# A two-layer trunk on one core: token groups of three tiles and two, a third expert pick begun between merge steps, first queries in two passes, and three gates of four on ScalarE in the expansion

## The reference, cut to what matters

```
x = LN(alpha*x + g1 * (sum_n sigmoid(h @ Wgate_n) * (branch_n @ Wbranch_n)) @ Wout)   # n = 3 branches
h = LN(x) * (1 + sc2) + sh2
q = h @ peer_wq                       # 8 heads x 2 halves x 64
sv, si = top_k(q . subkeys, 16)       # per head and half, 128 keys each
cand = sv[0][:,None] + sv[1][None,:]  # 256 sums, the 16 best are the experts
gates = softmax(best 16)
out = sum over 8*16 experts of gate * gelu(h . u[e]) * v[e]
x = LN(alpha*x + g2 * out)
```

## Time and profile before

| | us |
|---|---|
| median of 3 runs | 4697.08 (4692.81 to 4699.29) |
| profiled execution, its own time | 4696.58 |
| its span, first to last instruction | 4694.8 |
| PE busy | 4083.7 (87%) |
| DVE busy | 3542.0 (75%) |
| ACT busy | 1482.1 (32%) |
| POOL busy | 2014.6 (43%) |

### The profile page before, as it was taken

One profiled execution on the slowest core, in us unless ns is written; L12 is line 12 of the kernel. 1 busy time (PEld: TensorE's weight loads), 2 busy tenths in 40 slices (PEclk: granted clock), 3 DMA queues, 4 the chain that ended last, 5 costly groups with the idle time before them and its releaser, 6 DMA issues.

```text
span 4694.8 us, 67028 instructions
## 1 busy us (share of the span) xinstructions
PE 4083.7 (87%) x23702; PEld 3584.3 (76%) x23702; DVE 3542.0 (75%) x6464; ACT 1482.1 (32%) x2065; POOL 2014.6 (43%) x1123
## 2 busy tenths in 40 slices
PE   6889999763799999999888999997448999999996
PEld 5866888753699888988777678887337988889885
DVE  2407447689899999999952263487898999999998
ACT  2226322222333332333232363232223333333331
POOL 1200313000287777877622004120004887778774
PEclk9999999887999999999988999998789999999998
DMA  5220332332699999999853104323228999999996
GB/s 219 108 96 1 135 148 99 131 108 81 223 401 403 383 394 372 408 394 396 329 199 135 51 19 153 130 108 127 84 81 311 403 396 398 393 373 405 389 396 250
DMA packets 334645, 1130.38 MB, mean 241 GB/s; under 512 B 26368, under 2 KB 124720, under 8 KB 277104
## 3 DMA queue, kind: packets, MB, share of 16 engines
q0 software_dynamic: 151168, 552.73, 30.4%
q1 hardware_dynamic: 83312, 519.61, 28.2%
q10 hardware_dynamic: 99968, 55.58, 3.9%
HBM read 1068.30 MB, written 59.51 MB: 240 GB/s over the span
## 4 chain that ended last, share of the span: by engine, by line
DVE 34%; PE 29%; POOL 10%; DVEq 10%; issue 9%; DMA 6%; ACT 2%; ACTq 0%; SPq 0%; POOLq 0%
PE PS L703 8%; DVE acc L2182 6%; DVE ring_lo L2152 5%; POOL got_a L678 5%; POOL got_b L678 5%; PE PS L712 4%; PE PS L713 4%; PE PS L714 4%; DVE ohB L2133 3%; DVEq L2174 3%; DMA ring<-weights 3%; DVE spare L2182 3%; PE PS L707 3%; DVEq L2159 3%; DVE got_b L2179 2%
## 5 line engine op out<-in xcount | busy, mean ns | idle before, releaser
L1509 ACT CAST ring_hi<-ring 128x2048 fp32r<-128x2048 f32 x256 | 489.7, 1913 | 1266.9 <-DMA ring<-weights 1266.9
L678 POOL DMA_INDIRECT got_a<-u_rows,sidx x256 | 426.5, 1666 | 866.0 <-DMA gate_matrix<-stg 768.2
L712 PE MATMUL PS<-hT_hi,ring_hi 128*128 128x384 f32 x2048 | 688.7, 336 | 14.2 <-DVE ring_lo L2152 14.2
L714 PE MATMUL PS<-hT_hi,ring_lo 128*128 128x384 f32 x2048 | 688.3, 336 | 0.0
L713 PE MATMUL PS<-hT_lo,ring_hi 128*128 128x384 f32 x2048 | 687.4, 336 | 0.0
L712 PE MATMUL PS<-ring_hi,W_hi 128*128 128x512 f32 x1536 | 607.5, 396 | 51.3 <-DVE W_lo L2168 51.3
L656 POOL TENSOR_TENSOR ring_lo<-ring,mhi 128x2048 fp32r<-128x2048 f32 x48 | 223.5, 4655 | 902.3 <-ACT mhi L1347 902.3
L713 PE MATMUL PS<-ring_lo,W_hi 128*128 128x512 f32 x1536 | 604.1, 393 | 0.0
L714 PE MATMUL PS<-ring_hi,W_lo 128*128 128x512 f32 x1536 | 604.1, 393 | 0.0
L2152 DVE TENSOR_TENSOR ring_lo<-ring,ring_hi 128x2048 fp32r<-128x2048 f32 x256 | 585.2, 2287 | 0.0
L678 POOL DMA_INDIRECT got_b<-v_rows,sidx x256 | 427.1, 1669 | 160.7 <-DVE acc L2182 90.2
(11 more groups left out here) (365 smaller groups left out, 8497.9 us busy)
## 6 DMA issues: line engine op xcount, KB each, us to landing
ring<-weights SPq DMA_DIRECT2D x444, 1024.0 KB, 7.7
G<-gate_matrix SPq DMA_DIRECT2D x128, 384.0 KB, 9.1
gate_matrix<-stg ACTq DMA_DIRECT2D x10, 4096.0 KB, 15.9
gate_matrix<-stg ACTq DMA_DIRECT2D x2, 3584.0 KB, 18.1
x_wait<-x POOLq DMA_DIRECT2D x2, 2560.0 KB, 23.0
x<-x_wait ACTq DMA_DIRECT2D x10, 512.0 KB, 10.0
lnr<-lnrows POOLq DMA_DIRECT2D x4, 1024.0 KB, 5.1
got_a<-u_rows,sidx POOLq DMA_INDIRECT x256, 9.0
```

Of the source, the lines that this page charges most:

```text
L678: pool.indirect_dma_start(out=got[n % GB], out_offset=None, in_=u_rows[:, :] if phase % 2 == 0 else v_rows[:, :], in_offset=bass.IndirectO ...
L712: mm(out, a_hi, b_hi, start=first, stop=False)
L714: return mm(out, a_lo, b_hi, start=False, stop=final)
L1509: nc.scalar.copy(ring_hi[s][:, :], ring[:, s, :]).then_inc(hi_ready, 1)
```

## The change

- The groups become three tiles and two: `TILES = ((0, 1, 2), (3, 4))`, so the first group has 384 columns and the second 256.
- In the second group gate and branch product of a merge share one bank, and merges 0 to 3 use banks 0 to 3 and need no `gated` between them. All four run before the transposes of the first group.
- Tile 2 joins tiles 0 and 1: its transposes, queries and scores are made inside the second group's merges. The first queries go in two passes over the same four weight blocks: tile 0 alone (128 columns), then tiles 1 and 2 (256). Only one pass (`WQB`, tiles 3 and 4) is left after the merges, and `WQC` with its four transfers is gone.
- On DVE the steps of the picks are numbered through (`hidden(n)`, 11 per tile). Steps 0 to 5 run after merge 3, 6 and 7 after merge 4, then one per merge. After merge 20 tile 2 has had steps 0 to 2; its steps 3 to 9 and `chosen` come after the second group's projection and normalisation.
- The copies of tiles 0 and 1 back to token order (`tokens_first`) move to merges 8 and 12.
- In the expansion DVE makes `ohB` with one comparison for three tokens and one compare-and-multiply for the fourth; ACT multiplies the three by their gates, two quads ahead of the copy (`gate_quad`). `ohB` has four buffers, so DVE may be four quads ahead of PE. PE waits for ACT's gates instead of DVE.

```diff
-TILES = ((0, 1), (2, 3, 4))
-FIRST = (0, 2)
-COLS = (2 * P, 3 * P)
+TILES = ((0, 1, 2), (3, 4))
+FIRST = (0, 3)
+COLS = (3 * P, 2 * P)
...
-                        for k in range(4):
-                            token = bass.ds(i * 16 + (4 * u + k), 1)
-                            last = ts_(ohB[:, u % 2, k, :], iota, idxT[:, 1, token], idxT[:, 2, token], ALU.is_equal, ALU.mult)
-                        last.then_inc(oh_ready, 1)
+                        others = idxT[:, 1, bass.ds(i * 16 + (4 * u + 1), 3)].unsqueeze(2).broadcast_to([P, 3, P])
+                        tt(ohB[:, u, 1:4, :], iota.unsqueeze(1).broadcast_to([P, 3, P]), others, ALU.is_equal)
+                        token = bass.ds(i * 16 + 4 * u, 1)
+                        ts_(ohB[:, u, 0, :], iota, idxT[:, 1, token], idxT[:, 2, token], ALU.is_equal, ALU.mult
+                            ).then_inc(oh_ready, 1)
...
+                        def gate_quad(i, q):
+                            act.wait_ge(oh_ready, l * N_QUAD + t * QUADS + i * 4 + (q + 1))
+                            for k in range(1, 4):
+                                token = bass.ds(i * 16 + (4 * q + k), 1)
+                                o = ohB[:, q % 4, k, :]
+                                last = A(o, o, ACT.Identity, scale=idxT[:, 2, token])
+                            last.then_inc(gated_ready, 1)
...
+                        with act.Fori(0, 4 - half) as i:
                             for u in range(4):
-                                act.wait_ge(quad_full, l * N_QUAD + t * QUADS + i * 4 + (16 * half + u + 1))
-                                nc.scalar.copy(st[:, :, bass.ds(i * 16 + 4 * u, 4)],
-                                               bank(4 + u).rearrange("p (t j) -> p j t", t=4)).then_inc(quad_ready, 1)
+                                gate_quad(i, 16 * half + u + 2)
+                                quad_out(i, u)
...
+                def hidden(n):
+                    t, b = n // 11, set_a
+                    step = n % 11
+                    if step == 0:
+                        best_eight(t, b, early)
+                    if step in (1, 2):
+                        found_eight(b, early, step - 1)
...
                 for j in range(24):
                     gated(1, j)
...
+                    if j == 3:
+                        for n in range(6):
+                            hidden(n)
+                    if j == 4:
+                        hidden(6)
+                        hidden(7)
+                    if 5 <= j < 13:
+                        hidden(j + 3)
+                    if j == 13:
+                        hidden(16)
+                    if j == 14:
+                        hidden(17)
+                        hidden(18)
+                    if 15 <= j < 21:
+                        hidden(j + 4)
...
+                for n in range(25, 32):
+                    hidden(n)
+                chosen(2, set_c, idx[:, 2, :]).then_inc(idx_ready, 1)
...
                 for j in range(24):
                     merge(1, j)
...
-                    if j == 1:
+                    if j == 3:
                         pe.wait_ge(row_ready, layer_at(l, 2, 2))
-                        ln_turn(1, xn2, TILES[0])
...
+                        ln_turn(1, xn2, (0, 1))
+                        pe.wait_ge(hT_ready, layer_at(l, N_HT, NT + 2))
+                        queries(WQA, 0, slice(0, P))
+                        pe.wait_ge(mg_done, layer_at(l, N_MG, 24 + 4))
+                        ln_turn(1, xn2, [2])
                         pe.wait_ge(q_ready, layer_at(l, N_Q, 4))
                         pe.wait_ge(keys_full, 16 * (l + 1))
                         score_early(0)
+                        pe.wait_ge(hT_ready, layer_at(l, N_HT, NT + 6))
+                        queries(WQA, 4, slice(P, 3 * P))
+                        pe.wait_ge(q_ready, layer_at(l, N_Q, 8))
+                        score_early(1)
```

More of the change, by code:

```diff
@@ L160, with group_of, out_step @@
     pm: object
+def group_of(t):
+    return 0 if t in TILES[0] else 1
+def out_step(group, k):
+    return (0, 4 * len(TILES[0]))[group] + len(TILES[group]) * k
 def layer_at(l, per_layer, n):
@@ L381, in bank, with ln_bank, query_at, merge_banks @@
             return PS[:, b * 512 + a:b * 512 + e]
+        def ln_bank(part, t, h):
+            return 4 + (2 * t + h) % 4 if part == 0 else (6, 4, 2, 0, 2)[t] + h
+        def query_at(j, size):
+            if j < 4:
+                return 6 + j // 2, 2 * size * (j % 2)
+            return (2 + j % 2 if j < 8 else j % 4), 0
+        def merge_banks(group, j):
+            n = COLS[group]
+            if group == 0:
+                return bank(2 * (j % 2), 0, n), bank(2 * (j % 2) + 1, 0, n)
+            b = j if j < 4 else j % 2
+            return bank(b, 0, n), bank(b, n, 2 * n)
         slot_full = [sem(f"slot_full{i}") for i in range(RING + 1)]
@@ L510, in trunk @@
             else:
-                last_use += merges[:HALF] + [(q_full, N_Q, k + 1) for k in range(4)] + merges[HALF:] + outs
+                last_use += merges[:HALF] + [(q_full, N_Q, 4 + k + 1) for k in range(4)] + merges[HALF:] + outs
         last_use += [(sc_full, NT, NT)]
-        last_use += [(q_full, N_Q, 4 + k + 1) for k in range(8)]
+        last_use += [(q_full, N_Q, 8 + k + 1) for k in range(4)]
         assert len(last_use) == PEER
@@ L1919, in _ @@
                 merged_lo(0, 7)
-                for j in range(8):
-                    if j == 6:
+                for j in range(12):
+                    if j == 9:
                         dve.wait_ge(ln1_rows, 16 * (l + 1))
@@ L2078, in pick @@
                     return chosen(t, set_b, gates)
+                def hidden(n):
[5 more added lines that the diff above has]
+                        found_eight(b, early, step - 1)
+                    if step == 3:
+                        next_eight(b)
+                    if step == 4:
+                        found_next(b)
+                    if step == 5:
+                        pair_sums(b)
+                    if step == 6:
+                        pairs_found(b)
+                    if step == 7:
+                        pairs_next(b)
+                    if step == 8:
+                        places(b)
+                    if step == 9:
+                        looked_up(t, b)
+                    if step == 10:
+                        listed(t)
@@ L2120, in _ @@
-                for t in others:
+                aggregate(TILES[1])
+                inverse_root(11, TILES[1])
+                for t in TILES[1]:
                     normalise(t, xn2[:, t - FIRST[1], :]).then_inc(xn_ready, 1)
-                with dve.Fori(0, ND) as t:
-                    pick(t + NS, idx[:, 2, :], l * ND + t + 1).then_inc(idx_ready, 1)
+                for n in range(25, 32):
+                    hidden(n)
+                chosen(2, set_c, idx[:, 2, :]).then_inc(idx_ready, 1)
```

261 lines of the change are left out of this document (124 added, 137 removed).

## The result

Before: 4698.18 us median (4692.81 to 4699.58, 4 runs). After: 4672.34 us (4666.48 to 4675.41, 4 runs). The ratio is 0.9946, 95% interval 0.9928 to 0.9963: faster by half a per cent. The profiled execution has a span of 4673.6 us against 4694.8, 21.2 less.

A forecast was written before the change was run, and what follows sets the result against it. DVE and PE were taken as nearly full in the merges, DVE as setting the expansion's pace. Terms summed to -11.8 us per layer, -23.6 for two, from 4696.6 to 4673 us; range 4640 to 4716.

The forecast's parts named there:

- Part 1, merges of group one: First group with three tiles: 24 merges at 6.74 us instead of 4.60, less one stall; +47.2 us per layer.
- Part 1, projection: First group's projection: 12 slices instead of 8, at 2.88 us each; +11.5 us per layer.
- Part 2, to merge 4: End of first projection to second group's merge 4, now with two query passes: +7.1 us per layer.
- Part 3, merges 4 to 23: Second group's merges, set by DVE's work plus stalls, not PE alone: -23.3 us per layer.
- Part 4, to the first one-hots: Merge 23 to the expansion: earlier, shorter projection and one query pass, 93.2 us for 129.5; -36.3 per layer.
- Part 5, expansion: Expansion quads at 1.38 us instead of 1.63, with three products on ACT: -18.0 us per layer.
- The stall of merge 3: First group: merge 3's 2.62 us wait for DVE's first gated work, and slower running after, goes; -4.2 us.
- The third pick's cast: After the last query pass: ACT's index cast, made after the query copies, is what comes late next.
- the stalls on DVE: Merges 4 to 23: DVE stalls from POOL's subtractions and ACT's cast, taken as 17 us per layer.
- rival C: Between second-group merges, POOL's eight subtractions hold DVE in full: 41 us instead of 17; 4721 us total, chance 0.14.
- The signs that I named: Second group: merges about 5.7 us apart, long adds about 14 us per layer; over 130 us from merge 4 refutes.
- Rival E: Second group's merges held by the ring of four, 11.8 us from merge end to use; 4699 us, chance 0.04.

The follow-up runs named there:

- case 7: Changed kernel with POOL's subtraction for group two cut into eight pieces of 256 columns: 4650.37 us, ratio 0.9904 to the kernel before.
- case 8: Changed kernel with POOL's subtraction for group two cut into two pieces of 1024 columns: 4662.17 us, ratio 0.9931 to the kernel before.
- case 6: Changed kernel with the gated product written back to PSUM, so the add has one input there: 4664.4 us, ratio 0.9936 to the kernel before.
- case 10: Changed kernel with eight-piece subtraction, first tile's steps 6-8 behind merge 3, third pick's steps 22-24 behind the projection: 4640.6 us, ratio 0.9884 to the kernel before.
- case 1: Changed kernel with all four expansion gates back on DVE, ohB keeping four buffers: 4704.41 us, ratio 1.0013 to the kernel before.
- case 3: Kernel before with four ohB buffers instead of two and nothing else: 4676.09 us, ratio 0.9958 to the kernel before.
- case 2: Kernel before with only the new expansion (three gates of four on ACT, four ohB buffers): 4645.89 us, ratio 0.9888 to the kernel before.
- case 4: Changed kernel with the old expansion (two ohB buffers, all gates on DVE), so the regrouping alone: 4711.45 us, ratio 1.0031 to the kernel before.
- case 9: Changed kernel with the first tile's pick steps 6 to 8 moved behind merge 3, where DVE idles: 4649.76 us, ratio 0.9903 to the kernel before.

## Why the prediction was right, and where not

The forecast was 4673 us with a range of 4640 to 4716; 4672.34 was measured. Its steps, per layer, against layer one of the trace (the second layer's regrouping cost 2.6 us more):

| step | predicted | measured |
|---|---|---|
| Part 1, merges of group one | +47.2 | +46.7 |
| Part 1, projection | +11.5 | +11.9 |
| Part 2, to merge 4 | +7.1 | +5.7 |
| Part 3, merges 4 to 23 | -23.3 | -13.8 |
| Part 4, to the first one-hots | -36.3 | -37.2 |
| Part 5, expansion | -18.0 | -23.7 |
| sum | -11.8 | -10.4 |

**Parts 1, 2 and 4** held to 1.4 us each (the merges, the projection, the passes). The stall of merge 3 went and nothing came in its place. The first query pass of 128 columns took 14.55 us, not the 17.0 of the earlier trace rows, with PE at full clock. The third pick's cast was the late step, as said: it starts at 986.23, when ACT has made the query copies, and from the last query pass to the first one-hot it stays 13.9 us.

**Part 3 failed in one term**, the stalls on DVE. The forecast put 17 us, 14 of them for holds and 3 for ACT's cast. Measured are 26.3 for holds and 2.9 for the wait behind the cast, 29.2 together. DVE's way from its first product (782.41) to the end of the add that lets merge 23 go (901.31) is 118.9 us; without the 29.2 it is 89.7, where the forecast had 92.8. So the stalls were 12.2 us too small and the work 3.1 too large, and with the start and the last merge, 0.4 together, that is the 9.5 us by which the stretch came out longer.

Where the 17 came from was wrong twice. The "measured 18" of the earlier trace rows counts the adds alone, and 21.9 us were held before already, one picking step with them. And I had argued that some holds would fall where DVE waits anyway. It was the other way: before, DVE waited 19.0 us for sigmoids in merges 4 to 23, and now only 2.9 behind merge 4, and seven of eight subtractions held something, for six of eight. In mechanism this is rival C, and at 29.2 us it stands just beyond the 29 from which that rival was to decide, although the total lies by the forecast. The signs that I named show it too: the stretch took 129.0 us, just under the 130 that would have made the prediction wrong, and a merge takes 6.5 us there and not 5.7. I also expected the excess in the adds alone, 14 us a layer, and they show (33.6 - 32 x 0.43) / 2 = 9.9; the rest sits in picking steps. Cases 7 and 8 show that the length of POOL's instruction sets the length of each hold, and that the sum falls much only with the eight short pieces; case 6 shows that a hold moves on when the held instruction is taken away. Rival E's wait was absent from this stretch, but appears once DVE is relieved (case 10).

**Part 5 was too small**, by a term that was left out and in spite of one that was too large. The pace was right, 1.36 us a quad against 1.38, and ACT set it, as forecast. Its worth is 93 x 0.27 = 25 us. But the gates as a whole gave 14.2 us (case 1) and not 18.0. DVE waited 7.3 us for PE in the last tile, behind ACT's casts, where the forecast had 4.4, and the next pick did not start earlier (-2.0 in the forecast): in two tiles DVE waits 5 us in all around its first steps. What I left out are the four buffers. I worked with 1.63 us for every quad of before and did not look at the waits at the edges of a tile (0.69 and 2.24 us in two rows of the timeline). Alone the buffers give 9.4 us a layer (case 3); after the regrouping, which takes 3.6 of it, 5.8.

So the total was right partly by luck: two errors, +9.5 and -5.7 a layer, nearly cancel, and so do some that were in no sum. Layer one started 2.4 us later, and what stands behind the expansion in each layer, costed at nothing, took 2.5 and 2.9 us less. The mechanism of the forecast, an expansion that pays for a regrouping that does not, is shown by cases 2 and 4.

By the rule of the Trainium skill, "ScalarE: Activation LUTs", section "What ACT_TABLE_LOAD costs", that I weighed, a product in a row would take 0.293 us, an estimate; the trace agrees, (1.01 - 0.41) / 2 = 0.30. For the modulation, where the rule gives 479 ns, the prediction names 469; the group of the trace before has a mean of 482. The advice to multiply on VectorE, in the same page's section "Rules for kernel authors", would have cost 14.2 us a layer here (case 1).

## What to carry to other kernels

Before work is moved into the gaps of an engine, sum what other engines do to it there, over all of its instructions and not over one line: an engine with slack can hide its holds, a full one pays them, and taking away the instruction that is held gives most of the wait to the next. Here it paid to cut the long instruction that does the holding into short pieces (case 7), or to put the work where the engine is idle (case 9). And when a change has two parts, run each alone: here one was worth 52 us and the other cost 16.

## What had not been expected

- Only some DVE instructions are held by POOL's subtraction. A run of FIND_INDEX8 went on at 0.26 us apiece inside one. In the changed kernel:

```profile
839.54 4.59 POOL L690 TENSOR_TENSOR ring_lo<-ring,mhi 128x2048 fp32r<-128x2048 f32 x1 [0.79 <-ACT mhi L1382]
```

```profile
839.99 0.28 DVE L2028 FIND_INDEX8 si_a<-sv_a,work_a 128x8 uint32<-128x128 f32 x1
```

- A copy of 8 columns, 0.17 us of work, is held as long as larger instructions: 4.28 us.
- Eight pieces of 256 columns cost POOL 5.7 us for 4.6, and a DVE instruction that meets them still loses 0.3 to 0.5 us each time.
